# Pooling splits amid the forward pass, the sum of the convolution's taps in PSUM, and the convolution norm's reciprocal in eight pieces

## The reference

```python
# first block, multiscale_pool: windows 2, 4, 8, 16, one for each quarter of the channels
parts.append((csg[:, hi + 1] - csg[:, lo]) / cnt - uf[..., sl])
d = jnp.stack(parts, axis=2)
y = jnp.einsum('blgc,gcd->blgd', d, w_pool.astype(jnp.float32)).reshape(B, L, POOL_W)
# first block, branch_out
o_n = rmsnorm(o, gla_norm_g).astype(zA.dtype).reshape(B, L, GLA_VW)
yB = (multiscale_pool(uB, w_pool, pool_scale) * jax.nn.silu(zB)) @ w_branch_b
# second block, convolution: 31 taps along the tokens, 256 channels
h = a * jax.nn.sigmoid(gate)
h = _dwconv(h, w, b)
h = _group_layernorm(h, ng, nb, CV_GROUPS)
return jax.nn.silu(h)
# second block, spatial gating
u = jax.nn.gelu(u)
v = _layernorm(jax.nn.gelu(v), ln_g, ln_b)
mixed = jnp.einsum("gpq,bnqgc->bnpgc", w_s, vr) + b_s.T[None, None, :, :, None]
return u * mixed.reshape(bn, ln, ch)
```

## Time and profile before

| | us |
|---|---|
| three runs | 2650.6, 2660.3, 2660.5 |
| median | 2660.3 |
| the profiled execution, as timed | 2659.4 |
| its span in the profile | 2657.6 |
| PE busy in the span | 2493.3 (94%) |
| DVE busy | 1516.2 (57%) |
| ACT busy | 731.2 (28%) |
| POOL busy | 1057.7 (40%) |

### The profile page before, as it was taken

One profiled execution on the slowest core, in us unless ns is written; L12 is line 12 of the kernel. 1 busy time (PEld: TensorE's weight loads), 2 busy tenths in 40 slices (PEclk: granted clock), 3 DMA queues, 4 the chain that ended last, 5 costly groups with the idle time before them and its releaser, 6 DMA issues.

```text
span 2657.6 us, 33035 instructions
## 1 busy us (share of the span) xinstructions
PE 2493.3 (94%) x12008; PEld 2042.5 (77%) x12008; DVE 1516.2 (57%) x2193; ACT 731.2 (28%) x1244; POOL 1057.7 (40%) x493
## 2 busy tenths in 40 slices
PE   8999999999999889999986999899799999999997
PEld 4888788888887768877765887677578888888885
DVE  5796156878511466537796544465864444444446
ACT  4411334444200354123232444432211111111112
POOL 2344333333376524467540111025554444444444
PEclk9999999999999989999996899899899999999998
DMA  9576455444576632434211223421111111111111
GB/s 353 183 252 247 146 166 153 151 155 151 196 274 253 258 140 95 140 111 133 89 54 44 80 70 89 152 86 56 57 56 47 47 48 48 47 47 47 47 47 72
DMA packets 131090, 324.72 MB, mean 122 GB/s; under 512 B 11553, under 2 KB 59233, under 8 KB 125473
## 3 DMA queue, kind: packets, MB, share of 16 engines
q1 hardware_dynamic: 91376, 215.90, 24.9%
q10 hardware_dynamic: 39600, 107.30, 11.3%
HBM read 248.04 MB, written 70.39 MB: 120 GB/s over the span
## 4 chain that ended last, share of the span: by engine, by line
PE 50%; DVE 8%; issue 3%; ACT 1%; DMA 1%; DVEq 0%; POOL 0%; SPq 0%; ACTq 0%
PE pb L483 36%; PE g L2994 6%; PE g L3067 2%; PE pb L2994 1%; DVE zcs L2261 1%; PE g L3047 1%; PE g L2975 1%; DVE f_spare L2470 1%; PE g L2854 1%; DVE xl L2173 1%; DMA kept_in<-cs_d 1%; PE g L2973 0%; DVE ml L2477 0%; DVE hl L2540 0%; DVE cb L2519 0%
## 5 line engine op out<-in xcount | busy, mean ns | idle before, releaser
L851 POOL TENSOR_TENSOR w_hi<-w_raw,one 128x1024 fp32r<-128x1024 f32 x191 | 398.8, 2088 | 1461.3 <-PE pb L483 1062.7
L854 POOL TENSOR_TENSOR w_lo<-w_raw,w_hi 128x1024 fp32r<-128x1024 f32 x191 | 516.2, 2703 | 14.9
L483 PE MATMUL pb<-xh,w_hi 128*128 128x512 f32 (+1 forms) x1224 | 474.8, 388 | 18.8 <-DVE zkr L2232 8.8
L483 PE MATMUL pb<-xh,w_lo 128*128 128x512 f32 (+1 forms) x1224 | 467.2, 382 | 0.0
L483 PE MATMUL pb<-xl,w_hi 128*128 128x512 f32 (+1 forms) x1224 | 467.0, 382 | 0.0
L483 PE MATMUL pb<-mh,w_hi 128*128 128x512 f32 x704 | 279.0, 396 | 16.0 <-DVE ml L2477 7.3
L483 PEld LDWEIGHTS pb<-xh,w_hi 128*128 128x128 f32 x1224 | 233.1, 190 | 66.9 <-issue 9.4
L483 PE MATMUL pb<-mh,w_lo 128*128 128x512 f32 x704 | 276.5, 393 | 0.0
L483 PE MATMUL pb<-ml,w_hi 128*128 128x512 f32 x704 | 276.1, 392 | 0.0
L483 PEld LDWEIGHTS pb<-xl,w_hi 128*128 128x128 f32 x1224 | 232.6, 190 | 44.2
L483 PEld LDWEIGHTS pb<-xh,w_lo 128*128 128x128 f32 x1224 | 233.1, 190 | 42.8 <-issue 0.7
(11 more groups left out here) (414 smaller groups left out, 4632.2 us busy)
## 6 DMA issues: line engine op xcount, KB each, us to landing
w_raw<-in_wall SPq DMA_DIRECT2D x190, 512.0 KB, 3.6
mod_later<-in_modw SPq DMA_DIRECT2D x28, 1024.0 KB, 6.2
proj_d<-stage ACTq DMA_DIRECT2D x40, 512.0 KB, 3.0
at_bias<-in_bias SPq DMA_DIRECT2D x64, 192.0 KB, 2.8
mod_raw<-in_modt SPq DMA_DIRECT2D x8, 1024.0 KB, 10.6
w_raw<-in_wall ACTq DMA_DIRECT2D x15, 512.0 KB, 6.5
svt<-vt_d ACTq DMA_DIRECT2D x11, 512.0 KB, 6.3
vc<-proj_d SPq DMA_DIRECT2D x10, 512.0 KB, 6.1
```

The source lines that it names most:

```text
L483: mm = pe.matmul(pb[bank][:, 0:n], w[:, b, wc:wc + P], x[:, k, tokens], start=(count == 0), stop=(count == total - 1))
L851: nc.gpsimd.tensor_tensor(w_hi[:, b, :], w_raw[:, b, :], one[:, 0:1].to_broadcast([P, 1024]), ALU.mult).then_inc(w_high, 1)
L854: nc.gpsimd.tensor_tensor(w_lo[:, b, :], w_raw[:, b, :], w_hi[:, b, :], ALU.subtract).then_inc(w_split, 1)
```

## The change

It has three parts, and moves some buffers to make room for them.

**Pooling.** The barrier at the end of the forward pass is gone. `q_high(0)` on ACT stands behind the eviction of step 4, the silus of group 0 (`q_silu(0)`, taken out of `q_gate`) behind that of step 5, `q_low(0)` on DVE behind the state update of step 5. `dl` now lies where `qd` lies, eight tiles instead of four. ACT's order after the pass is `q_high(1)`, the squares of head 0 into a buffer of their own, `osq_first`, then for each group `q_gate`, `q_high` of the group after next, `q_silu` of the next. `o_means(0)` on PE stands between the products of groups 0 and 1.

**Convolution and gating.** The sum of the taps is in `g[0:4]` (`conv_sum`); the last tap reads it there and writes `zcs`. The gating's transposes, which used those banks, now use `g[4:6]`, in two turns of four token blocks: the first before `T_PAIR`, the second behind it. The eight `ctx_low` and their inputs on ACT stand before the taps and behind the first tile of `T_SG`. The four small matmuls with `sgw_sb` stand before `T_SG`. The multiplication of `sg_b` (L2271) stands before the first `memset` of `hpad`. Where the steps of the gating's norm and the low parts stand among the taps is shown in the diff.

**Attention.** The reciprocal is taken in eight pieces of 128x256, in steps 0, 2, 3, 4 and 5 (`POWERS_AT`), and the multiplications are one step later, in steps 5 and 6.

```diff
+        dh = [at("dh0", [P, 2, T], arena + 136 * 1024, F32R)[0], at("dh1", [P, 2, T], arena + 149 * 1024, F32R)[0]]
...
+        dl, _ = at("dl", [P, 8, T], arena, F32R)
...
+        POWERS_AT = {0: (0, 1), 2: (2, 3), 3: (4,), 4: (5, 6), 5: (7,)}
...
-            sp.wait_ge(y_act, 2)
+            sp.wait_ge(y_act, 3)
...
+            def q_high(grp):
+                if grp >= 2:
+                    act.wait_ge(unit_done, UNIT[T_POOL] + 4 * grp - 4)
+                act.wait_ge(q_in[grp], 16)
+                for n in (2 * grp, 2 * grp + 1):
+                    act.activation(dh[grp % 2][:, n % 2, :], qd[:, n, :], ACT.Copy).then_inc(q_dh, 1)
+            def q_silu(grp):
+                for n in (2 * grp, 2 * grp + 1):
+                    act.wait_ge(q_z[n % 2], 16 * (n // 2 + 1))
...
                         (pb[n][:, :] if c % 2 == 0 else g[:, 4 + n, :]).rearrange("p (t n) -> p t n", n=CH),
...
+                if c == 4:
+                    q_high(0)
+                if c == 5:
+                    q_silu(0)
...
             def q_gate(grp):
-                for n in (2 * grp, 2 * grp + 1):
-                    act.wait_ge(q_z[n % 2], 16 * (n // 2 + 1))
-                    act.activation(zb[:, n % 2, :], zb[:, n % 2, :], ACT.Silu).then_inc(q_sil, 1)
...
-            act.wait_ge(u_d, 17)
-            q_high(0)
-            for grp in range(1, 4):
-                q_high(grp)
-                q_gate(grp - 1)
...
-            def o_squares(h):
-                act.activation(osq[:, :, :], pair_of(oall, h), ACT.Square).then_inc(o_sq, 1)
+            def o_squares(h, squares=osq):
+                act.activation(squares[:, :, :], pair_of(oall, h), ACT.Square).then_inc(o_sq, 1)
...
-            act.wait_ge(q_dl, 8)
+            act.wait_ge(u_d, 17)
+            q_high(1)
+            act.wait_ge(f_oev, NCX + 1)
+            o_squares(0, osq_first)
+            for grp in range(3):
+                q_gate(grp)
+                if grp < 2:
+                    q_high(grp + 2)
+                q_silu(grp + 1)
+            act.wait_ge(unit_done, UNIT[T_POOL] + 4)
             o_load_za(0)
             q_gate(3)
-            o_squares(0)
             act.wait_ge(unit_done, UNIT[T_B])
...
             for t in range(4):
                 read_out(T_SG + t, zcs[:, 4 + t, :], ACT.Gelu_apprx_tanh)
-                for k in (3 * t, 3 * t + 1, 3 * t + 2):
-                    if k < KT:
-                        act.wait_ge(t_ready, 5 * KT + k + 1)
-                        act.activation(xh[:, k, T:TA], ctx_raw[:, k, :], ACT.Identity,
-                                       bias=modc[:, 24 + k:25 + k]).then_inc(xh_ready, 1)
+                for k in range(KT) if t == 0 else ():
+                    act.wait_ge(t_ready, 5 * KT + k + 1)
+                    act.activation(xh[:, k, T:TA], ctx_raw[:, k, :], ACT.Identity,
+                                   bias=modc[:, 24 + k:25 + k]).then_inc(xh_ready, 1)
...
-            act.wait_ge(y_pe, 2)
-            for n in range(NCX):
-                v = act.activation(vtok[:, n, :], g[:, n // 2, C * (n % 2):C * (n % 2) + C], ACT.Copy,
-                                   accum_out=vstat[:, 0, n:n + 1])
-            v.then_inc(y_act, 1)
-            pair_k_high(0, 0, pair_unit(u_k))
-            act.wait_ge(y_dve, 1)
+            def gating_tokens(first):
+                act.wait_ge(y_pe, 2 + first // 4)
+                for n in range(4):
+                    v = act.activation(vtok[:, first + n, :], g[:, 4 + n // 2, C * (n % 2):C * (n % 2) + C], ACT.Copy,
+                                       accum_out=vstat[:, 0, first + n:first + n + 1])
+                v.then_inc(y_act, 1)
+            gating_tokens(0)
+            for n in range(3):
+                pair_k_high(0, n, pair_unit(u_k + n))
+            gating_tokens(4)
+            act.wait_ge(y_dve, 2)
...
-            act.wait_ge(y_act, 2)
+            act.wait_ge(y_act, 3)
             act.activation(vstat[:, 1, :], vstat[:, 1, :], ACT.Sqrt, scale=1.0 / C,
                            bias=epsc[:, 0:1]).then_inc(y_act, 1)
-            for n in (1, 2):
-                pair_k_high(0, n, pair_unit(u_k + n))
...
                         stf[:, 1 - b, h, :], stf[:, b, h, :], dec[:, c, h:h + 1],
                         g[:, 2 * b + h // 2, DV * (h % 2):DV * (h % 2) + DV], ALU.mult, ALU.add)
                 u.then_inc(f_upd, 1)
-            end_phase(dve, 4)
...
+                if c == 5:
+                    q_low(0)
...
-            q_low(0)
-            for grp in range(1, 4):
-                q_low(grp)
-                q_gate(grp - 1)
-            q_gate(3)
+            dve.wait_ge(u_d, 17)
+            q_low(1)
+            for grp in range(4):
+                if grp == 1:
+                    for n in range(U_BUFS):
+                        dve.wait_ge(u_out[n], 64)
+                q_gate(grp)
+                if grp < 2:
+                    q_low(grp + 2)
...
+            nc.vector.tensor_scalar(vstat[:, 3, 0:2], col[:, COL["sg_b"]:COL["sg_b"] + 2], float(C), None, ALU.mult)
...
+            def conv_sum(t):
+                return g[:, 2 * t:2 * t + 2, :].rearrange("p a n -> p (a n)")
             for t in range(2):
-                nc.vector.tensor_scalar(zcs[:, t, :], hpad[:, t, 0:T], col[:, cw + TAPS * t:cw + TAPS * t + 1],
+                nc.vector.tensor_scalar(conv_sum(t), hpad[:, t, 0:T], col[:, cw + TAPS * t:cw + TAPS * t + 1],
                                         col[:, cbias + t:cbias + t + 1], ALU.mult, ALU.add).then_inc(z_cv, 1)
...
                         nc.vector.scalar_tensor_tensor(
-                            zcs[:, t, :], hpad[:, t, bass.ds(tap, T)],
+                            conv_sum(t), hpad[:, t, bass.ds(tap, T)],
                             col[:, bass.ds(tap + (cw + TAPS * t), 1)],
-                            zcs[:, t, :], ALU.mult, ALU.add).then_inc(z_cv, 1)
+                            conv_sum(t), ALU.mult, ALU.add).then_inc(z_cv, 1)
             u_k, u_v, u_q, u_k1, _ = PAIR_UNITS
-            taps(1, 5)
             for k in range(KT):
                 ctx_low(k)
-            taps(5, 14)
-            nc.vector.tensor_scalar(vstat[:, 3, 0:2], col[:, COL["sg_b"]:COL["sg_b"] + 2], float(C), None, ALU.mult)
...
             dve.wait_ge(y_pe, 1)
             for t in range(2):
-                nc.vector.scalar_tensor_tensor(sgb_sb[:, t, :], g[:, 4, P * t:P * t + P], vstat[:, 3, t:t + 1],
-                                               sgb_sb[:, t, :], ALU.mult, ALU.add)
-            for n, (first, last) in enumerate(((14, 17), (17, 18), (18, 20))):
+                v = nc.vector.scalar_tensor_tensor(sgb_sb[:, t, :], g[:, 4, P * t:P * t + P], vstat[:, 3, t:t + 1],
+                                                   sgb_sb[:, t, :], ALU.mult, ALU.add)
+            v.then_inc(y_dve, 1)
+            taps(1, 15)
+            for n, (first, last) in enumerate(((15, 17), (17, 18), (18, 20))):
                 pair_k_low(0, n, pb[(u_k + n) % 2], bank_free[(u_k + n) % 2])
                 taps(first, last)
-            dve.wait_ge(y_act, 3)
+            dve.wait_ge(y_act, 2)
+            nc.vector.tensor_scalar(vstat[:, 0, :], vstat[:, 0, :], -1.0 / C, None, ALU.mult).then_inc(y_dve, 1)
+            taps(20, 24)
+            dve.wait_ge(y_act, 4)
             nc.vector.reciprocal(vstat[:, 1, :], vstat[:, 1, :]).then_inc(y_dve, 1)
-            dve.wait_ge(y_dve, 2)
+            dve.wait_ge(y_dve, 3)
             nc.vector.tensor_tensor(vstat[:, 2, :], vstat[:, 0, :], vstat[:, 1, :], ALU.mult).then_inc(y_dve, 1)
-            for n, (first, last) in enumerate(((20, 23), (23, 25))):
+            for n, (first, last) in enumerate(((24, 27), (27, 29))):
                 taps(first, last)
                 pair_q_low(0, n, pb[(u_q + n) % 2], bank_free[(u_q + n) % 2])
-            taps(25, TAPS)
+            taps(29, TAPS - 1)
+            for t in range(2):
+                dve.wait_ge(z_cv, 2 * TAPS - 3 + t)
+                nc.vector.scalar_tensor_tensor(
+                    zcs[:, t, :], hpad[:, t, TAPS - 1:TAPS - 1 + T], col[:, cw + TAPS * t + TAPS - 1:cw + TAPS * t + TAPS],
+                    conv_sum(t), ALU.mult, ALU.add).then_inc(z_cv, 1)
...
-                at_q = zcs[:, 2 + q // 2, H * (q % 2):H * (q % 2) + H]
-                nc.vector.reciprocal(at_q, at_q).then_inc(z_dve, 1)
+                at_q = zcs[:, 2 + q // 4, C * (q % 4):C * (q % 4) + C]
+                v = nc.vector.reciprocal(at_q, at_q)
+                if q % 2:
+                    v.then_inc(z_dve, 1)
...
-                if s < 4:
-                    conv_power(s)
-                if s in (4, 5):
-                    conv_scaled(s - 4)
+                for q in POWERS_AT.get(s, ()):
+                    conv_power(q)
+                if s in (5, 6):
+                    conv_scaled(s - 5)
...
-            end_phase(pe, 4)
+            pe.wait_ge(f_oev, 8)
+            def o_means(h, squares=osq):
```

(69 more changed lines are left out.)

46 lines of the change are left out of this document (15 added, 31 removed).

## The result

The kernel after takes 2616.6 us (median of four runs, 2615.4 to 2619.4), the kernel before 2655.5 beside it (2644.7 to 2660.5): a ratio of 0.986, interval 0.982 to 0.990. Against the profiled execution of before, from which the prediction counts, that is 42.8 us; 26.9 were forecast. (Between the two medians it is 38.8 us; the profiled execution of before was among its slower ones, which will matter.)

A forecast was written before the change was run, and what follows sets the result against it. It took TensorE to bound the kernel, with DVE the only other engine of weight. Pooling 8.1, taps 18.0 and attention 0.8 made 26.9 us, from 2659.4 to 2632.5 us; range 2619 to 2646 (own range 2624 to 2642).

The forecast's parts named there:

- Pooling: From forward pass to `T_B`: early group 0 split and silus, moved `o_means(0)`, start `T_B` 8.1 us earlier; bounds 4 to 13.
- Taps: Convolution's taps, to the last tap: 18.0 us less on DVE, with PE's queries ending earlier; range 12 to 22.
- The meetings with POOL: In the 60 taps: contention of two-SBUF-input DVE instructions with POOL, 14.5 us, removed by putting the sum in PSUM.
- The price of PSUM: In 58 taps: reading and writing the sum in PSUM costs zero, between -0.03 and +0.1 us an instruction.
- the rival at 2702: Taps: reading and writing one PSUM bank takes turns, 1.2 us more a tap, 70 us for 58; chance 0.05.
- half the cure: Taps: meetings with POOL don't depend on where the sum lies, so 14.5 us of gain is gone: 2647; chance 0.07.
- The first tap of each half: Convolution: loses its fast form and takes 1.2 us each, where two took 1.54: +0.9 us.
- the wait for the parts of the keys: PE in the taps' stretch: 8.8 us of waiting for the keys' low parts, queued behind taps on DVE, goes.
- the 6 to 12 that I gave: Sign in the profile after: PE's wait for the last tap is 6 to 12 us instead of 18.4.
- Attention, the failed step: Attention's reciprocals: step 1 loses PE's 1.11 us wait for `osb`, step 5 costs +0.3; sum -0.8 us.
- the low clock of attention has another length: Attention's start: a change in how long PE's clock is low was listed as showing the prediction wrong.
- the clock of attention: Attention: if PE's step 1 gap kept the clock low, it returns four steps early, 7.6 us more: 2625; chance 0.08.

The follow-up runs named there:

- that one line undone: The kernel after with `conv_sum` returning `zcs` again, so the taps' sum lies in SBUF, every order and wait kept: 2653.9 us.

## Why the prediction was wrong

**Pooling, right in sum.** Forecast 8.1 us, kept to the end; the medians give 6.2. From the end of the forward pass to `T_B` it was 55.3 us in the profile before and 53.0 and 54.9 in the other two executions, against 43.2 after: 10 to 12 us, more than forecast, since DVE's order took 38.4 us from its first product to the last `bl` instead of my 40.5 (it was 38.5 and 40.3 in the other two executions of before, where nothing was changed), and the gating began 4.4 us behind the forward pass, not 6.9. What I missed is the other side: "after it the stage `T_B` is PE's own, so the gain lasts" left out that moving `o_means(0)` away lets the clock fall at the head of `T_B`, 2.3 us.

**Taps, right.** Forecast -18.0 from `T_CV` to the last tap; it is 170.8 us before, 152.7 after: -18.1. The meetings with POOL were 14.5 in the sum and 86.7 - 72.4 = 14.3 in the trace. The price of PSUM, written as zero with -0.03 to +0.1 us, is 0.00 to 0.01 a tap (median 1281 against 1275 ns, with the sum read from and written to the same two banks), so the rival at 2702 was wrong, and so was the one at 2647 (half the cure). The first tap of each half lost 1.1 us instead of 0.9. PE's queries ended at 1379.5, well ahead of 1388: the wait for the parts of the keys is gone, as forecast, and of the new waits only 3.4 us for the values are there. The stand of 8.2 us lies in the 6 to 12 that I gave.

**The bound from POOL's side, not seen.** I counted the taps' sum in SBUF as a loss of DVE's. The kernel with that one line undone shows that this would have been the smaller loss of the new order: POOL stood, and PE behind it, 24.2 us.

**Attention, the failed step.** "Only in step 1 does PE wait because of it: 1.11 us [...] Sum -0.8." Measured: 15.9 us from the means to the end. Two things are in it.

- The reciprocals, 6.2 to 7.5 us. I read the slack of each step from an execution in which PE ran those steps at half its clock. There DVE had time. At full clock steps 1 and 3 wait 4.6 us for `osb`, behind a reciprocal of 3.34 us, and the clock falls again behind the wait. The term was mis-sized because a slack was taken as a property of the kernel when it was one of the clock.
- The low clock, 9.8 us. "The steps' form is what it was", so I held its length for constant. It isn't constant even in the kernel before: 41 us in one execution, 10 in two others. So these 9.8 us are no gain of the change over a short execution of before. That the profile's 2659.4 lay at the upper end of three runs spread over 10 us was there to be read, and "the low clock of attention has another length" was among the prediction's own signs of being wrong.

The rival "the clock of attention" named the right stretch, with 7.6 us of price, but the wrong cause. In both short executions of the kernel before PE waits in step 1 for 3.0 us, longer than the 1.11 of the long one, and the low clock lasts 10 us all the same; it is back by the beginning of step 1, before that wait.

Sum against the profile before: 8.1 + 18.0 + 0.8 forecast; in spans 6.1 up to `T_CV` (with the forward pass's +3.3 in it), 18.1 and 15.9 measured. Against the two short executions (2646.1 and 2646.3 us) the kernel after is 29.5 to 29.6 us faster: of the 42.8, 13.3 lie between executions of the unchanged kernel, 9.8 behind the means and 3.5 ahead of them. Had the prediction started from such an execution, its 26.9 us would have missed by only 2.7, and that by luck: in spans the three parts are 3.0, 17.6 and 6.1 us from there, against 8.1, 18.0 and 0.8 forecast (the profiled execution of after was 2.8 us slower than its median).

Open is what sets the length of the low clock, and why two executions of one kernel differ in it; shown is only that the length goes with the place of the fall beside PE's wait. What was tried excludes the length of the stand as such, the clock level at the means and the reciprocals' places.

## What to carry to other kernels

Before slack is read from one profile, look at the granted clock of the stretch: slack of another engine beside a slowed TensorE is not there at full clock. Where a kernel's own runs spread by more than a term of the sum, take a second profile of the unchanged kernel before pricing anything near the stretch that varies. And a wait of TensorE that can't be removed may be filled with products of constants into a free bank: in the kernel after this kept the clock and gave 3.6 us behind the means, in the kernel before, with the stand alone filled, it gave nothing (2650.4 us beside 2648.5). The step that is moved away from such a wait may have been doing that.

## What the runs showed of the hardware

- VectorE instructions of two SBUF inputs, back to back, held one GpSimd instruction of 1.9 us for 32.18 us, and lost next to nothing themselves (1.199 us each). In the kernel before such meetings cost both sides (13.72 us for a split, up to 3.42 for a tap).
- Reading and writing the same two PSUM banks in one VectorE instruction of 128x1024 takes 1.28 us, as in SBUF (1.275; 1.28 with the sum read from PSUM and written to SBUF). The Trainium skill's higher fixed cost for a PSUM source ("VectorE: DVE Perf Modes", "The TRN2 errata") doesn't show at this size.
- Beside one and the same wait of PE (2.6 to 3.0 us), with the same products behind it, the granted clock stayed at 1.2 GHz for 10, 17 or 41 us, and for two of these lengths (10 and 41) in executions of one unchanged kernel. In the profile before PE was busy for all of 10 us at the low clock and for 28.9 of the 30 after them, and the clock was still low for most of that time (0.50 and 0.55).
